# All eight half units of the last output block in a row, the router's work for both token tiles behind them

## What is computed

```python
merged = (gates[:, :, 0] * (y_a @ w_br_a[l]) + gates[:, :, 1] * (y_b @ w_br_b[l])
          + gates[:, :, 2] * (y_c @ w_br_c[l]))
x = x + merged @ w_out[l]
x = x + moe_ffn(rms_norm(x, norm_ffn[l]), w_router[l], b_router[l], ...)
# moe_ffn: logits = xt @ w_router + b_router; top 4 of 32, softmax over the four;
#          g = min(xt @ w_gate[e] + b_gate[e], 7); u = clip(xt @ w_up[e] + b_up[e], -7, 7)
#          y += weight * (((u + 1) * g * sigmoid(1.702 * g)) @ w_down[e] + b_down[e])
```

## Time and profile before

| | us |
|---|---|
| median of 3 runs | 1469.82 |
| lowest, highest | 1469.2, 1473.81 |
| the profiled execution | 1471.5 |
| its span, first to last instruction | 1469.7 |

### The profile page before, as it was taken

How to read it: one execution, slowest core, us unless ns; L and a number is a source line. 1 busy time by engine, 2 the same in 40 slices (tenths; PEclk the granted TensorE clock), 3 DMA queues, 4 the chain that set the end, 5 groups by cost and what they waited for, 6 DMA issues and landing times.

```text
span 1469.7 us, 18622 instructions
## 1 busy us (share of the span) xinstructions
PE 1432.5 (97%) x7575; PEld 825.7 (56%) x7575; DVE 581.8 (40%) x1134; ACT 406.5 (28%) x601; POOL 101.3 (7%) x65
## 2 busy tenths in 40 slices
PE   6999998999999999999999999999999999999998
PEld 6998787877787874444444444444444444433443
DVE  6768786777788663111211112112111121211111
ACT  5766565554644441101001011011010100101010
POOL 5112421111100000000000000000000000000000
PEclk9999999999999999999999999999999999999999
DMA  7455434564454969999999999999999999999997
GB/s 247 152 187 174 142 116 143 179 189 156 151 213 170 323 257 427 423 429 428 428 429 429 428 428 428 429 429 428 429 429 428 428 429 429 429 428 428 428 427 299
DMA packets 74001, 491.28 MB, mean 334 GB/s; under 512 B 5264, under 2 KB 8976, under 8 KB 49376
## 3 DMA queue, kind: packets, MB, share of 16 engines
q1 hardware_dynamic: 71280, 487.57, 82.2%
q10 hardware_dynamic: 2160, 2.62, 0.6%
q0 software_dynamic: 512, 0.43, 0.1%
HBM read 488.93 MB, written 1.07 MB: 333 GB/s over the span
## 4 chain that ended last, share of the span: by engine, by line
PE 83%; DMA 10%; DVE 5%; issue 1%; ACT 1%; DVEq 0%; ACTq 0%; SPq 0%
PE ps L1929 25%; PE ps L1967 14%; DMA regions<-in_w_up 9%; PE ps L1590 8%; PE ps L1591 8%; PE ps L1592 8%; PE ps L1857 7%; PE ps L1577 4%; PE ps L1909 3%; PE ps L1804 1%; DVE splits L1037 1%; PE ps L1937 1%; DMA halves<-in_w_br_a 1%; PE ps L1960 1%; DVE regions L1165 1%
## 5 line engine op out<-in xcount | busy, mean ns | idle before, releaser
L1929 PE MATMUL ps<-regions,sig 128*64 128x512 f32 x2048 | 463.3, 594 | 4.1 <-DMA regions<-in_w_gate 3.9
L1929 PEld LDWEIGHTS ps<-regions,sig 128*64 128x64 f32 x2048 | 142.1, 137 | 276.2 <-issue 259.8
L1967 PE MATMUL ps<-regions,tmp 128*64 128x512 f32 x1024 | 225.1, 592 | 0.0
L1590 PE MATMUL ps<-splits,regions_r 128*128 128x512 f32 x512 | 206.7, 404 | 1.7 <-DVE regions_r L1030 1.7
L1591 PE MATMUL ps<-splits,regions_r 128*128 128x512 f32 x512 | 200.8, 392 | 0.0
L1592 PE MATMUL ps<-splits,regions_r 128*128 128x512 f32 x512 | 200.7, 392 | 0.0
L724 ACT ACTIVATE splits<-halves 128x1024 fp32r<-128x1024 f32 x152 | 159.1, 1056 | 100.8 <-PE ps L1592 84.1
L1037 DVE TENSOR_TENSOR splits<-halves,splits 128x1024 fp32r<-128x1024 f32 x123 | 155.9, 1272 | 59.3 <-ACT splits L724 58.0
L910 ACT ACTIVATE work<-work 128x512 f32<-128x512 f32 x32 | 20.1, 629 | 474.8 <-DVE work L1517 474.8
L1967 PEld LDWEIGHTS ps<-regions,tmp 128*64 128x64 f32 x1024 | 71.8, 137 | 131.9 <-issue 129.4
L1857 PEld LDWEIGHTS ps<-craw,regions 128*128 128x128 f32 x1024 | 119.2, 192 | 25.6 <-issue 25.2
(11 more groups left out here) (299 smaller groups left out, 1207.7 us busy)
## 6 DMA issues: line engine op xcount, KB each, us to landing
regions<-in_w_gate SPq DMA_DIRECT2D x64, 2048.0 KB, 28.8
regions<-in_w_up SPq DMA_DIRECT2D x64, 2048.0 KB, 27.1
regions<-in_w_down SPq DMA_DIRECT2D x64, 2048.0 KB, 29.9
halves<-in_w_in SPq DMA_DIRECT2D x48, 1024.0 KB, 5.3
halves<-in_w_br_b SPq DMA_DIRECT2D x8, 1024.0 KB, 5.1
halves<-in_w_mem_kv SPq DMA_DIRECT2D x8, 1024.0 KB, 5.0
halves<-in_w_br_a SPq DMA_DIRECT2D x4, 1024.0 KB, 7.5
halves<-in_w_br_c SPq DMA_DIRECT2D x4, 1024.0 KB, 7.5
```

What stands on the lines that cost most here:

```text
L1590: pe.matmul(out, lhs[0], rhs[0], start=start, stop=False, skip_group_check=True)
L1929: last = pe.matmul(ps[64 * h:64 * h + 64, bank, :], xgT[:, 4 * k + c], eslots[slot][:, c, h * NB:(h + 1) * NB], start=(k == 0 and c == 0), ...
L1967: last = pe.matmul(ps[64 * h:64 * h + 64, D_BANK, :], actT[:, c, 64 * k:64 * k + 64], eslots[slot][:, c, h * NB:(h + 1) * NB], start=False ...
```

## The change

The half units of the second tile move from behind the list into it: quarters 0 and 1 behind the first tile's quarter 1, quarters 2 and 3 behind its quarter 3. "outT" and "logits" move behind all eight. On VectorE, `add_out(0)`, the whole root of tile 0 (`norm_begin(0)`, the new `norm_end(0)`) and `add_out(1)` move ahead of the two copies of "outT". The root of tile 1 moves ahead of `choose(0)`. `turn_out(0)` joins "outT", and `turn_out(1)` comes right behind `last_logits(0)`. `last_logits(1)` and `open_sum(1, 0)` move ahead of the place count of tile 0. `second_tile`, `turn_out`, `add_out`, `take_xT` and `norm_begin` are only moved in the text. `norm_end` is the part of `choose` that finished the root.

```diff
@@ schedule
-    at(first("wo", 1) + 2, "outT")
-    at(first("wo", 1) + 3, "logits")
+    for q in range(2):
+        at(first("wo", 1) + 1, "second", q)
+        at(first("wo", 1) + 3, "second", q + 2)
+    at(UNITS, "outT")
+    at(UNITS, "logits")
@@ VectorE
+            def norm_end(t):
+                inverse_root(rs_2[:, t:t + 1]).then_inc(sem("second_norm"), 1)
+                dve.wait_ge(sem("second_norm"), t + 1)
...
                 elif kind == "outT":
+                    add_out(0)
+                    norm_begin(0)
+                    norm_end(0)
+                    add_out(1)
                     for c2 in range(2):
...
             def choose(t):
-                inverse_root(rs_2[:, t:t + 1]).then_inc(sem("second_norm"), 1)
-                dve.wait_ge(sem("second_norm"), t + 1)
                 dve.wait_ge(sem("logits_ready"), t + 1)
...
-            add_out(0)
             take_xT(0)
-            norm_begin(0)
+            norm_begin(1)
+            norm_end(1)
             choose(0)
-            add_out(1)
             take_xT(1)
-            norm_begin(1)
             find_first(0)
             choose(1)
@@ TensorE
+                elif kind == "second":
+                    second_tile(step[1])
...
                     for c2 in range(2):
                         by_columns(lambda t: x_sb[:, t], c2)
+                    turn_out(0)
...
-            second_tile(0)
-            turn_out(0)
-            second_tile(1)
             last_logits(0)
-            second_tile(2)
-            second_tile(3)
-            pe.wait_ge(gemm_taken, GEMM_AT[("wo", 1, 0)] + 1)
+            turn_out(1)
+            pe.wait_ge(gemm_taken, GEMM_END)
             open_sum(0, 0)
-            turn_out(1)
+            last_logits(1)
+            open_sum(1, 0)
 
             b = group()
             pe.wait_ge(sem("chosen_ready"), 1)
             pe.matmul(ps[:, b, 0:EXPERTS], upto_r[:], chosen_r[:, 0], start=True, stop=True).then_inc(misc_ready, 1)
-            pe.wait_ge(gemm_taken, GEMM_END)
-            open_sum(1, 0)
-            last_logits(1)
```

More of the change, by code:

```diff
@@ L985, in rstd_here, with add_out, take_xT, norm_begin @@
                 return last
+            across = [P, TOP_K, EXPERTS]
+            def add_out(t):
+                n = GEMM_AT[("wo", 1, t)]
+                if t == 0:
+                    dve.wait_ge(sem("wo_first_tile"), 1)
+                else:
+                    dve.wait_ge(unit_used, UNITS)
+                dve.tensor_tensor(x_sb[:, t, NB:2 * NB], x_sb[:, t, NB:2 * NB], ps[:, GEMM_BANKS[n % 4], :], ALU.add)\
+                    .then_inc(gemm_taken, 1)
+            def take_xT(t):
+                b = group()
+                dve.tensor_copy(xT[:, 4:8, t * P:(t + 1) * P], ps[:, b, :].rearrange("p (c t) -> p c t", c=4))\
+                    .then_inc(misc_taken, 1)
+            def norm_begin(t):
+                dve.wait_ge(sem("out_squares"), TT + t + 1)
+                link(dve.tensor_tensor(ss_2[:, t:t + 1], ss_part[:, t:t + 1], ss_part[:, TT + t:TT + t + 1], ALU.add))
+                variance(rs_2[:, t:t + 1], ss_2[:, t:t + 1], D)
+            def norm_end(t):
+                inverse_root(rs_2[:, t:t + 1]).then_inc(sem("second_norm"), 1)
+                dve.wait_ge(sem("second_norm"), t + 1)
             dve.wait_ge(sem("masks"), 3)
@@ L1599, in router, with second_tile, turn_out @@
                 return last
+            def second_tile(q):
+                w = first("wo", 1) + q
+                hi, lo = quarter(w)[1:]
+                b = GEMM_BANKS[GEMM_AT[("wo", 1, 1)] % 4]
+                for c in range(2):
+                    k = 2 * q + c
+                    last = three_passes(ps[:, b, :], (mergedT[0][:, k, P:T], mergedT[1][:, k, P:T]),
+                                        (hi[:, c], lo[:, c]), k == 0, k == KC - 1)
+                last.then_inc(unit_used, 1)
+            def turn_out(t):
+                b = group()
+                pe.wait_ge(gemm_taken, GEMM_AT[("wo", 1, t)] + 1)
+                for c in range(4):
+                    last = turn(ps[:, b, c * P:(c + 1) * P], x_sb[:, t, (4 + c) * P:(5 + c) * P])
+                last.then_inc(misc_ready, 1)
             pe.wait_ge(sem("masks"), 3)
@@ L1826, in _ @@
                         by_columns(lambda t: merged[:, t], c2)
-            def second_tile(q):
-                w = first("wo", 1) + q
-                hi, lo = quarter(w)[1:]
-                b = GEMM_BANKS[GEMM_AT[("wo", 1, 1)] % 4]
-                for c in range(2):
-                    k = 2 * q + c
-                    last = three_passes(ps[:, b, :], (mergedT[0][:, k, P:T], mergedT[1][:, k, P:T]),
-                                        (hi[:, c], lo[:, c]), k == 0, k == KC - 1)
-                last.then_inc(unit_used, 1)
-            def turn_out(t):
-                b = group()
-                pe.wait_ge(gemm_taken, GEMM_AT[("wo", 1, t)] + 1)
-                for c in range(4):
-                    last = turn(ps[:, b, c * P:(c + 1) * P], x_sb[:, t, (4 + c) * P:(5 + c) * P])
-                last.then_inc(misc_ready, 1)
             def last_logits(t):
```

## The result

The kernel is slower: 1484.44 us, median of four executions (1483.22 to 1485.6), against 1471.16 for the kernel before in the same session (four, 1469.2 to 1473.81). The ratio is 1.0094 [1.0081, 1.0108]. The forecast of 1472.4 missed, and so did its range, which ended at 1477.0. Of the 12.0 us between forecast and median, 1.3 lie in the starting point: the forecast was set on 1469.8, the median of three executions of the kernel before, and with the fourth it is 1471.16. The profiled execution took 1483.2, its span grew from 1469.7 to 1481.4, or 11.7 us; the other 1.6 of the 13.3 between the medians lie in which execution was profiled (1.2 under its median here, 0.3 over it before).

A forecast was written before the change was run, and what follows sets the result against it. The stream of expert loads was taken to set the end, with load (2, 2) tied to the expert loop's start. Loop 3.8 us later less 1.2 slack gave +2.6 on 1469.8, so 1472.4 us, range 1468.8 to 1477.0.

The forecast's parts named there:

- The load (1, 0): Expert weight load goes out at 536.9 instead of 542.8 us; worth nothing by itself.
- The hole: TensorE ahead of the router: idle 2.15 us, 543.45 to 545.6, until VectorE's copies, held up by the root's table load.
- Router and choice of tile 0: Behind the hole: router products done at 548.3, tile 0's choice at 550.2 us.
- The order's price, X = 3.8: From the out products to the expert loop: the new order starts the loop 3.8 us later; bounds 3.0 to 4.3.
- The slack of 1.2 us: Load (2, 2), waiting for expert 0's down product: 8.7 less 7.5 us to spare, so the end moves 1.2 less.
- Whether the clock falls: TensorE's clock behind the 2.15 us hole: stays at 1.00 in the forecast (0.50); a fall got 0.25.
- What a fall costs: Behind the hole: 6 to 7 us at half rate, 24 router records taking 2.5 us more, loop 6.3 later, end +5.1.
- Rival A: Behind the hole near 543.4 us: the clock drops for 6 to 7 us, end +5.1, 1474.9; chance 0.25.
- B: Chain from out products to expert loop is shorter than worked out: loop 1 to 2 us later, about 1470; chance 0.17.
- C: Load stream: load (1, 0), 5.9 us earlier, brings all loads sooner, 1463.9; chance 0.05.
- D: Row of second-tile half units: a wait for splits or merged rows breaks the order, 1473; chance 0.03.

The follow-up runs named there:

- e6: Kernel before with only the second tile's quarters 0 and 1 moved into the list, so load (1, 0) goes out sooner; 1469.89 us, ratio 0.9995.
- e12: Changed kernel with large filler products: two in the hole ahead of the router, one ahead of `last_logits(1)`, others in three upstream waits; 1471.59 us, ratio 0.9995.
- e5: Changed kernel with 512-column filler products: two ahead of the router, two ahead of `last_logits(1)`, one ahead of each gather's wait; 1477.29 us, ratio 1.0038.
- e10: Kernel before with extra 512-column products in three waits far upstream, nothing moved; 1467.27 us, ratio 0.9978.
- e4: Kernel before with four extra 128x512 products, 3.4 us in all, ahead of the second gather; 1475.4 us, ratio 1.003.
- e1: Changed kernel with two extra 128x512 products in the hole ahead of the router products; 1474.65 us, ratio 1.003.
- e9: Changed kernel with eight small products of 32 columns in the hole ahead of the router products; 1482.97 us, ratio 1.0087.
- e11: Changed kernel with four extra 128x512 products in a row behind `open_sum(1, 0)`; 1481.9, 1481.9 and 1485.5 us, ratio 1.0095, a fourth execution of 2953.57 left out.

## Why the prediction was wrong, step by step

Times of the changed kernel are given less the 0.6 us by which its anchor is late (526.35 against 525.75).

- **The load (1, 0)** at 536.9: measured 536.9, and worth nothing, as said (e6). Right.
- **The hole:** 2.15 us, from 543.45 to 545.6, ended by the copies; measured 1.91, ended at 545.6. Right in place and cause. The copies wait for the root and the root for the table load, as worked out.
- **Router and choice of tile 0:** done at 550.2; measured 550.3 (550.88 less 0.6). Right.
- **The order's price, X = 3.8:** e12 gives 4.9, or about 3.7 less what its low stretch cost, e5 4.7 with about 1 of overshoot. About right; both subtractions are estimates. At full clock the end rose by 2.2 (e12's four executions over e10), close to the forecast's 2.6, but between two sessions, and less than 3.7 without slack would give; which of the two holds is open.
- **The slack of 1.2 us:** wrong term, small. It measured 0.3 in e4, and none on average over the ten traces with a late loop. The reading "8.7 less 7.5" looked at one load; in the changed kernel (2, 2) landed 8.2 behind its issue and the end moved 0.4 more than the loop.
- **Whether the clock falls:** the step that failed first. I judged the hole by its length against two others, 2.47 us (falls) and 1.73 (does not), and gave the fall 0.25. Each was one draw, and the neighbours were left out: from the row of large products ahead of it to the row behind it the 1.73 us hole has only eight transposes beside it, 2.8 us in all, while behind the 2.47 us hole stand 16 products of 64 columns, 5.9 us in all. Of the traces here, the clock fell behind the 2.4 us hole near 149 us in ten of twelve that have it, behind one of 1.7 to 1.9 us near 446 in six of twelve, and behind the 1.73 us hole at the anchor in none of fourteen. In the changed kernel all four executions have the low mean clock, with a hole of 1.91 us between twelve transposes and 24 router records. The Trainium skill ("TensorE: Matmul & The Clock Gate", "HAM oscillation — how this bites in real kernels") speaks of idle stretches; e1 agrees with it, e9, with nothing idle above 0.20 us, shows that small products count as well.
- **What a fall costs:** the step that made the miss large. Rival A took 6 to 7 us at the low clock, as in the earlier trace rows, with 24 router records in it, 2.5 us. Measured: 20.5 us, and those 24 records are not in it at all (2.87 us, full rate); what is in it is all that comes after. The second gather started at 561.4 for a forecast 557.0: 4.4 us. From it to the loop 5.41 us (562.01 to 567.42) for a forecast 2.87: 2.5 us. So 6.9 us in place of 2.5, of which I can name 1.67 for each of the two gathers (3.67 against 2.00) and 0.8 for `last_logits(1)` (1.91 against 1.08); the rest lies in the four `open_sum`, the place products and the handovers. The 6.8 us of the earlier trace rows ended 3.0 us behind the start of a row of large products (154.56 us). Here no such row came for 18 us, only the pairs of `open_sum`, and e11 shows that it is this that holds the clock down.

The sum as it came out: 3.8 for the order, 6.9 for the clock, no slack: +10.7 at the loop, then +0.4 to the end and +0.6 upstream, 11.7. The 6.9 is what is left of the loop's 10.7 once 3.8 is taken off; against e12 and e5, where the clock was mostly or wholly kept, it would be 5.8 to 6.0. Of the rivals, A named the right event at the right place, with the wrong condition for it (a hole's length) and the wrong price, 1474.9; B, C and D did not happen. What pointed to it was in the diff and the trace of before: the change takes 24 large products from between the small ones and leaves no row of them between 543 us and the loop.

Open are the cause of the single execution of 2953.57 us in e11, which load takes back the slack in e4, how much of the 6.9 us is the order's, and why the same stretch lets the clock fall in one execution and not in the next.

## What to carry to other kernels

Before small products are put together, look at what large ones stood between them: on TensorE, count the thin stretches (idle time and small products together), not the holes alone, and price a fall up to the next row of large products, not by the length that a fall had elsewhere. Where an engine must wait there, fill the wait with products of full width whose result nobody reads; narrow ones don't help. A kernel whose executions spread by several us with mean clocks just under 1.00 may have such waits, and filling them can be worth more than a reordering: here 2.7 us of 1470.

## What the runs showed of the hardware

- The clock's level has a memory: the same mixture of small products ran at 0.50 in the changed kernel and at 1.00 in e11 once four large products had raised it (0.50 until 557.0, 1.00 from there on).
- Filler of 512 columns in the hole spares eight of ten executions the long fall (e1), the same time filled with 32 columns none of four (e9), going by the mean clocks, though the profile calls PE busy in both.
- A long fall ends with the next row of large products: 2.3 to 3.0 us into the expert loop in five traces, whether it had lasted 13.7 us or 27.3; 1.3 us into the burst of e11.
- The same stretch of code lets the clock fall in one execution and not in another (six of twelve traces near 446 us). With the upstream waits filled (e10) the spread shrinks from 5.8 us to 2.0.
